# Gathering the sorted places of a mixture-of-experts stage in three segments, with two unread products in place of five

## The reference, cut to what matters

```
g_idx = top 1 of 4 groups;  e_idx = top 2 of the group's 8 experts
gate = softmax(two values) * softmax(groups)[g_idx]
order = argsort(expert)                    # 544 places: 272 tokens, two experts each
for each of the 32 experts, on its own tokens:
    a, u = split(x @ w_up[e]);  y = (silu(a) * u) @ w_down[e]
h[token] += y * gate
```

## Time and profile before

| | us |
|---|---|
| median of 3 runs | 2919.0 |
| the three runs | 2915.11, 2919.0, 2919.03 |
| the profiled execution, its own time | 2915.67 |
| its span, first instruction to last | 2913.9 |
| TensorE busy | 2689.0 (92%) |
| VectorE busy | 1461.7 (50%) |
| ScalarE busy | 776.3 (27%) |
| L1270 busy, 128 of its 192 products | 24.5 |

### The profile page before, as it was taken

One profiled execution on the slowest core, in us unless ns is written; L12 is line 12 of the kernel. 1 busy time (PEld: TensorE's weight loads), 2 busy tenths in 40 slices (PEclk: granted clock), 3 DMA queues, 4 the chain that ended last, 5 costly groups with the idle time before them and its releaser, 6 DMA issues. The chain is left out here.

```text
span 2913.9 us, 45820 instructions
## 1 busy us (share of the span) xinstructions
PE 2689.0 (92%) x18838; PEld 1921.8 (66%) x18838; DVE 1461.7 (50%) x3312; ACT 776.3 (27%) x1476; POOL 0.2 (0%) x4
## 2 busy tenths in 40 slices
PE   5999897999999998899999999999989999999998
PEld 4998776899899777799777743333346784333333
DVE  4885774687786475575233423333332633333333
ACT  4332253333433153433233211111112331111110
POOL 0000000000000000000000000000000000000000
PEclk9999898999999898999999999999999999999999
DMA  7776420576576420265321289999972135999997
GB/s 302 277 272 233 158 74 2 203 289 255 194 274 260 147 102 31 87 246 194 110 73 58 88 324 427 427 427 428 428 308 87 59 145 220 415 427 427 428 427 297
DMA packets 72025, 701.58 MB, mean 241 GB/s; under 512 B 8704, under 2 KB 11136, under 8 KB 11392
## 3 DMA queue, kind: packets, MB, share of 16 engines
q1 hardware_dynamic: 71808, 698.54, 60.0%
HBM read 697.46 MB, written 1.05 MB: 240 GB/s over the span
## 5 line engine op out<-in xcount | busy, mean ns | idle before, releaser
L1528 PE MATMUL ps<-arena_parts 128*128 128x256 f32 x2112 | 603.7, 286 | 24.1 <-DVE arena_parts L3218 24.1
L1530 PE MATMUL ps<-arena_parts,ring_parts 128*128 128x256 f32 x2112 | 600.6, 284 | 0.0
L1529 PE MATMUL ps<-arena_parts 128*128 128x256 f32 x2112 | 598.6, 283 | 0.0
L1300 PE MATMUL ps<-ring,arena 128*64 128x512 f32 x2048 | 467.1, 598 | 0.3 <-DMA ring<-slabs 0.3
L1528 PEld LDWEIGHTS ps<-arena_parts 128*128 128x128 f32 x2112 | 402.5, 191 | 25.5 <-issue 25.3
L1530 PEld LDWEIGHTS ps<-arena_parts,ring_parts 128*128 128x128 f32 x2112 | 410.5, 194 | 0.0
L1529 PEld LDWEIGHTS ps<-arena_parts 128*128 128x128 f32 x2112 | 402.9, 191 | 0.2
L833 PE MATMUL ps<-h,ring 128*128 128x256 f32 (+1 forms) x1536 | 375.3, 404 | 19.4 <-DVE h L2561 10.0
L833 PEld LDWEIGHTS ps<-h,ring 128*128 128x128 f32 x1536 | 303.0, 200 | 74.5 <-issue 10.9
L3132 DVE TENSOR_TENSOR ring_parts<-ring,arena_parts 128x2048 fp32r<-128x2048 f32 x132 | 299.4, 2289 | 74.1 <-ACT arena_parts L1690 74.1
L1690 ACT CAST arena_parts<-ring 128x2048 fp32r<-128x2048 f32 x132 | 249.6, 1904 | 317.4 <-DMA ring<-slabs 310.3
(11 more groups left out here) (409 smaller groups left out, 2477.5 us busy)
## 6 DMA issues: line engine op xcount, KB each, us to landing
ring<-slabs SPq DMA_DIRECT2D x190, 2048.0 KB, 14.6
ring<-slabs SPq DMA_DIRECT2D x278, 1024.0 KB, 5.0
sq<-aside SPq DMA_DIRECT2D x2, 1024.0 KB, 8.5
arena<-aside SPq DMA_DIRECT2D x2, 1024.0 KB, 10.5
x<-xT SPq DMA_DIRECT2D x1, 1024.0 KB, 8.7
outT<-x SPq DMA_DIRECT2D x1, 1024.0 KB, 4.6
constants<-const SPq DMA_DIRECT2D x1, 1004.5 KB, 6.3
vectors<-vec SPq DMA_DIRECT2D x1, 747.5 KB, 4.3
```

The lines of the kernel that those rows point to most:

```text
L1300: mm = nc.tensor.matmul(ps[W * hh:W * hh + W, e % 2, :], xe[:, e % 2, 4 * k + c], wt[:, c], start=(k == 0 and c == 0), stop=(k == 1 and c ...
L1528: nc.tensor.matmul(out, w_hi, v_hi, start=start, stop=False, skip_group_check=True)
L1529: nc.tensor.matmul(out, w_hi, v_lo, start=False, stop=False, skip_group_check=True)
L1530: return nc.tensor.matmul(out, w_lo, v_hi, start=False, stop=stop, skip_group_check=True)
```

## The change

The 544 places are gathered in three segments: 0 to 127, 128 to 271, 272 to 543. The first is gathered before the experts. The second follows up_part(1, 1), all 8 blocks at once. The third follows behind experts 1 and 2, in two pieces of 4 blocks. VectorE places three segments instead of two halves. ScalarE's order for the first three experts changes: expert 2's gather comes behind the copies of the second segment, expert 3's ahead of silu_e(2), and expert 4's behind the last copies, as before. keep_clock ahead of the first expert issues two matmuls instead of five.

```diff
-PIECES = (range(0, 3), range(3, 6), range(6, KC))
+SEGMENTS = ((0, P), (P, T2), (T2, SLOTS))
+PIECES = ((1, range(KC)), (2, range(0, 4)), (2, range(4, KC)))
...
             def gather(q, half, mark_at, wait_at, banks, ks=range(KC)):
+                lo_slot, end = SEGMENTS[half]
...
-                            mm = nc.tensor.matmul(bank(banks[(k - ks[0]) % 4], T2), rows_of[0:size, t, k * P:(k + 1) * P],
-                                                  pm[0:size, t, half * T2:(half + 1) * T2], start=(t == 0 and w == 0),
-                                                  stop=(t == 2 and w == 1))
+                            mm = nc.tensor.matmul(bank(banks[(k - ks[0]) % 4], end - lo_slot),
+                                                  rows_of[0:size, t, k * P:(k + 1) * P], pm[0:size, t, lo_slot:end],
+                                                  start=(t == 0 and w == 0), stop=(t == 2 and w == 1))
...
                 def combine(e):
                     if e < 2:
-                        await2("act", q, "xs", 1, PIECES[e + 1][-1])
+                        await2("act", q, "xs", 2, PIECES[e + 1][1][-1])
...
-                keep_clock(2, 5)
+                keep_clock(2, 2)
...
                         elif e == 1:
-                            await2("act", q, "xs", 1, PIECES[0][-1])
+                            await2("act", q, "xs", 1, KC - 1)
...
-                        gather(q, 1, mark2, lambda engine, *key: (await2 if engine == "act" else await_)(engine, *key),
-                               (4, 5, 6, 7), PIECES[e])
+                        gather(q, PIECES[e][0], mark2,
+                               lambda engine, *key: (await2 if engine == "act" else await_)(engine, *key), (4, 5, 6, 7),
+                               PIECES[e][1])
...
             def take_sorted(q, half, mark_at, wait_at, banks, ks=range(KC)):
-                    if half == 1 and k == 0:
+                    if half == 2 and k == 0:
                         await_("dve", q, "xpad")
-                    mark_at(nc.scalar.copy(xs[:, k, half * T2:(half + 1) * T2], bank(banks[(k - ks[0]) % 4], T2)), q, "xs", half, k)
+                    lo_slot, end = SEGMENTS[half]
+                    mark_at(nc.scalar.copy(xs[:, k, lo_slot:end], bank(banks[(k - ks[0]) % 4], end - lo_slot)),
+                            q, "xs", half, k)
...
                 for e in range(NE):
-                    if 2 <= e and e + 1 < NE:
+                    if e == 1:
+                        gather(3)
+                    if e + 1 < NE:
                         silu_e(e + 1)
-                    if e == 2:
-                        take_sorted(q, 1, mark2, await2, (4, 5, 6, 7), PIECES[2])
-                        await2("act", q, "xs", 1, KC - 1)
-                    if e + 2 < NE:
+                    if e < 3:
+                        take_sorted(q, PIECES[e][0], mark2, await2, (4, 5, 6, 7), PIECES[e][1])
+                        await2("act", q, "xs", PIECES[e][0], PIECES[e][1][-1])
+                    if e != 1 and e + 2 < NE:
                         gather(e + 2)
-                    if e < 2:
-                        silu_e(e + 1)
-                        take_sorted(q, 1, mark2, await2, (4, 5, 6, 7), PIECES[e])
                     take_y(e)
...
             def place(q, half):
-                io = cst("iota", half * T2, T2)
+                lo_slot, end = SEGMENTS[half]
+                io = cst("iota", lo_slot, end - lo_slot)
...
-                    pm = part(PM, 3, SLOTS)[0:size, t, half * T2:(half + 1) * T2]
+                    pm = part(PM, 3, SLOTS)[0:size, t, lo_slot:end]
...
                 place(q, 1)
+                place(q, 2)
```

## The result

The changed kernel takes 2938.0 us, the median of five runs (2922.5 to 2942.3); the kernel before takes 2918.4, also of five (2910.5 to 2919.0). The ratio is 1.0067 with a 95% interval from 1.0049 to 1.0086: slower by 19.6 us (14 to 25 by the interval), where 9.9 was forecast. The sign is right and the size is not; 2938.0 lies above the forecast range of 2918 to 2935.

The account below looks back on a forecast made before the run. TensorE was taken to bound each expert stage until the weight stream is unbroken, transfers afterwards. Stages of +5.05 and +4.85 gave +9.9 us, put on 2917.4: 2927.3 us, range 2918 to 2935.

Parts of the forecast that it names:

- The bound: Expert stages: TensorE sets the pace up to about 2490 us in the second, then weight transfers at 428 GB/s.
- The price of a group: Gather's six products per k: 0.96 us at 128 columns, 0.97 at 144, 1.13 at 272, with a 0.112 weight floor.
- B: Rival: gather price goes by columns, so gathers are only moved; 2914.4 us, the same; chance 0.06.
- C: Rival: no weight floor for gather products, a group 0.76 or 0.80 us; 2921.3 us, within 0.2%; chance 0.12.
- the figure of the Trainium skill: Gather: about 81 ns a product at 128 columns, weights loaded each time; group some 0.83 us, sum about +5.5.
- The moved work: VectorE's three more place pairs and ScalarE's later expert gathers stay covered, costing nothing; uncovered, up to 3 and 2.1 us each.
- The clock: First stage: a slow stretch falls on real products, costing 1.8 us; late gathers had stayed at 1.00.
- Rival D: Narrow 128-column gathers drop the clock to 1.2 GHz, 1.8 us each time; 2931 or 2934.5 us; chance 0.19.
- The forecast's 3.6 us: Slow part of the first stage's ten unread records, which took 4.18 us against 2.5 at full clock.
- 5.05: Second stage's net us: -1.38 first gather, -1.37 unread products, +7.8 second segment.
- the forecast's 1.8 for a slow stretch: First stage: cost in us if the slow clock stretch comes as before and lies on real products.
- 4.85: First stage's net us: start 2.95 earlier, then +7.8 for the second segment's gather.

Follow-up runs that it names:

- before_extra: Kernel before, with the second half's 48 gather products of 272 columns issued once more, unread, behind expert 0 of each stage: 2932.6 us, ratio 1.0070.
- The turned order: Kernel before, every other block k taking its token tiles as 2, 1, 0: 2909.4 us; with two unread products instead of five as well: 2905.8 us.
- after_again: The changed kernel once more, no edit, against the kernel before: 2935.3 us, ratio 1.0077.
- after_wide: Changed kernel with the same three segments, but every gather product streaming 272 columns: 2927.2 us, ratio 1.0052 to the kernel before.
- after_split: Changed kernel with the second segment in two pieces of four groups, turn(0) and up_part(1, 1) between them: 2927.8 us, ratio 1.0051 to the kernel before.
- after_keep5: Changed kernel with five unread products again instead of two: 2939.2 us, ratio 1.0093 to the kernel before.
- after_turned: Changed kernel with every other block k taking its token tiles as 2, 1, 0, one change of partitions a group: 2926.1 us, ratio 1.0041 to the kernel before.

## Why the prediction was wrong in size and right in sign

**The bound** was read rightly. Up to the end of the starving TensorE's time counts nearly whole (before_extra: 18.2 added, 18.6 measured). Of the 10.9 and 11.1 us by which the eleventh load was issued late, 9.9 and 10.2 are left where the twentieth lands, and their sum, 20.1, is near the 19.6.

**The price of a group** at full clock was right: 0.95 and 0.97 us measured, 0.96 and 0.97 forecast, and 4.55 for four groups of the third segment, 1.14 each, as in the earlier trace rows. So B (price by columns, 0.53) and C (no floor of the weights, 0.76) are out. The starts of the single products in the changed kernel's trace show the floor directly: at full clock no two products of the 128-column gather start less than 0.11 us apart, twice the 0.053 that their columns take. The turned order bears out the other half of that price: with one change of partitions fewer in a group, 1.41 us went in eight groups, 0.18 each, near the 0.20 taken.
By the figure of the Trainium skill (its page "TensorE: Matmul & The Clock Gate", section "Back-to-back issue gap") that spoke against the floor, 81 ns a product, a group would take some 0.83 us, an estimate. The copies 0.95 us apart do not bear it out for these float32 weights.

**The moved work** cost next to nothing, as argued: in the second stage TensorE waits once, 0.19 us for ScalarE's gather for expert 0, and not for those of experts 2 and 4.

**The clock is the step that failed.** The sum had it fall at most once, for 1.8 us in the first stage, on the ground that it had stayed at 1.00 under the late gathers. Those were gathers of 272 columns, and their row says nothing of narrow ones. Rival D had the right mechanism at 0.19, but its size came from one short fall; each of the four real ones lasts 10 us. (The forecast's 3.6 us is a slip too: 4.18 less 2.5 is 1.7 us lost, so about 3.4 us were slow.) Put together for the second stage, over the forecast: first gather 9.69 for 7.68, +2.0; unread products with what stands around them 2.37 for 2.66, -0.3; up products of expert 0, 8.51 for 7.02, +1.5; second segment 10.19 for 7.8, +2.4; down_part(0) 5.73 for 3.5, +2.2. In all +7.8. The gather itself began 1.7 us earlier against the aside load, because here the slow stretch of the earlier trace rows at 2408 did not occur. 5.05 + 7.8 - 1.7 = 11.1, and the eleventh ring load was issued 11.1 us later. The first stage closes in the same way: from the gather's start to the first expert 12.80 for 10.25 (14.56 before, 4.31 less by the forecast), +2.5; up products 7.84 for 8.82 (the forecast's 1.8 for a slow stretch is in it), -1.0; second segment 10.63 for 7.8, +2.8; down_part(0) 5.18 for 3.5, +1.7. In all +6.1, and 4.85 + 6.1 = 10.9, as the eleventh load shows. So the clock, put at 1.8 us in the first stage and at nothing in the second, measured 7.9 (1.8 + 6.1) and 7.8 in this execution.

**That narrow products are the cause** rests first on three runs: the falls repeat (after_again), they are not there when only the width is changed (after_wide), and they are mostly not there when the stretch is cut up by dense products (after_split). The other traces agree: the clock falls within each of the 18 unbroken gathers of 48 narrow products in the five traces that have them, and within none of the 18 of 48 products with 272 columns in the seven others. The cause is not the cut of unread products (after_keep5). Nor does the fall need all of the stalls at changes of partitions (after_turned).

Widths between 144 and 272 columns were not run, and what of the fall is due to the weights and what to the remaining change of partitions is open. The median of the changed kernel moved between 2935.3 and 2938.0, and that of the kernel before between 2911.9 and 2918.4, which is as much as the forecast's 0.2%, so the split of the 19.6 us to single microseconds holds for the profiled execution and no further.

## What to carry to other kernels

In these kernels, cutting the columns of a matmul saved time only down to what its weights and the changes of partitions cost, and a long stretch of such narrow products cost the clock, for the products behind them too. Before splitting a gather into narrow pieces, ask for the price of a product at zero columns, and put narrow pieces between dense ones. Ordering the products so that neighbours have the same number of partitions gained 1.41 us in 48 products and cost nothing.

## What had not been expected of the hardware

- The granted clock goes to 0.50 for 10 us, 4 to 5 us into 48 products of 128 or 144 columns with 128-column weights (changed kernel; 3 to 5 in after_keep5), while TensorE shows as busy for 10.00 of 10.00 us. The same 48 products with 272 columns hold 1.00 (after_wide).
- Half clock does not double the time of these products: a group goes from 0.95 to 1.66 us, 1.75 times.
- The kernels without narrow products have stretches at half clock too. In the whole profile before they add up to 228 us, and their sum ahead of the first expert stage, which no edit touches, is 164 to 188 us from one profile to the next. A difference of 24 us at half clock can cost up to 12 us (an estimate), about as much as executions of one kernel differ.
